# One unread product ahead of the up-projections of three feed-forward layers, and another order of products in the last chunks of the first

## What is computed

```python
def swiglu(x, w1, w3, w2):
    return (jax.nn.silu(x @ w1) * (x @ w3)) @ w2
...
        h = layer_norm(DN_ALPHA * h + m, ln_g[i, 0], ln_b[i, 0])
        h = layer_norm(DN_ALPHA * h + swiglu(h, ffn_w1[i], ffn_w3[i], ffn_w2[i]), ln_g[i, 1], ln_b[i, 1])
```

## Time and profile before

| | us |
|---|---|
| median of 3 runs | 1177.24 |
| lowest and highest | 1177.13, 1178.37 |
| span of the profiled execution, first to last instruction | 1173.9 |
| PE busy in it | 1157.0 |
| DVE, ACT, POOL busy in it | 818.7, 600.6, 160.6 |

### The profile page before, as it was taken

One profiled execution on the slowest core, in us unless ns is written; L12 is line 12 of the kernel. 1 busy time (PEld: TensorE's weight loads), 2 busy tenths in 40 slices (PEclk: granted clock), 3 DMA queues, 4 the chain that ended last, 5 costly groups with the idle time before them and its releaser, 6 DMA issues.

```text
span 1173.9 us, 20445 instructions
## 1 busy us (share of the span) xinstructions
PE 1157.0 (99%) x8266; PEld 1037.8 (88%) x8266; DVE 818.7 (70%) x1263; ACT 600.6 (51%) x947; POOL 160.6 (14%) x212
## 2 busy tenths in 40 slices
PE   9999999999999999999999999999999999999996
PEld 7997899999877789999998889999979988999996
DVE  7789899989868687455466785454577768655554
ACT  6777444544445456354434565444438664544441
POOL 0650199003960000000000000000010000000000
PEclk9999999999999999999999999999999999999999
DMA  6676454555765558565544557555536334755540
GB/s 250 219 280 220 145 202 157 198 180 180 219 176 191 183 192 307 171 216 190 187 162 161 197 200 231 198 181 196 180 125 228 116 111 159 269 195 183 195 147 36
DMA packets 63974, 221.02 MB, mean 188 GB/s; under 512 B 8068, under 2 KB 9988, under 8 KB 63368
## 3 DMA queue, kind: packets, MB, share of 16 engines
q1 hardware_dynamic: 57224, 202.57, 50.7%
q0 software_dynamic: 5648, 15.73, 4.0%
q10 hardware_dynamic: 1008, 1.41, 0.4%
HBM read 211.03 MB, written 7.60 MB: 186 GB/s over the span
## 4 chain that ended last, share of the span: by engine, by line
PE 88%; DVE 8%; DMA 2%; ACT 1%; issue 1%; SPq 0%; DVEq 0%; ACTq 0%
PE bank L1627 15%; PE bank L1628 15%; PE bank L1629 15%; PE bank L1636 8%; PE bank L1642 8%; PE bank L1638 8%; PE bank L1747 5%; PE bank L1681 4%; DVE wlo L1020 2%; DMA raw<-in_w 2%; PE bank L1936 1%; PE bank L1607 1%; PE bank L1782 1%; PE bank L1918 1%; PE bank L1947 1%
## 5 line engine op out<-in xcount | busy, mean ns | idle before, releaser
L1020 DVE TENSOR_TENSOR wlo<-raw,whi 128x1024 fp32r<-128x1024 f32 x227 | 287.4, 1272 | 57.0 <-ACT whi L616 55.9
L616 ACT ACTIVATE whi<-raw 128x1024 fp32r<-128x1024 f32 x227 | 238.9, 1056 | 71.8 <-PE bank L1642 41.0
L1627 PE MATMUL bank<-xboth,whi 128*128 128x256 f32 x936 | 264.2, 282 | 0.0
L1628 PE MATMUL bank<-xboth,whi 128*128 128x256 f32 x936 | 262.3, 280 | 0.0
L1629 PE MATMUL bank<-xboth,wlo 128*128 128x256 f32 x936 | 262.3, 280 | 0.0
L1020 DVE TENSOR_TENSOR ext<-raw,ext 128x1024 fp32r<-128x1024 f32 x142 | 172.2, 1222 | 39.0 <-ACT ext L616 38.7
L1629 PEld LDWEIGHTS bank<-xboth,wlo 128*128 128x128 f32 x936 | 178.7, 191 | 0.0
L1627 PEld LDWEIGHTS bank<-xboth,whi 128*128 128x128 f32 x936 | 176.0, 188 | 2.5 <-issue 0.9
L1628 PEld LDWEIGHTS bank<-xboth,whi 128*128 128x128 f32 x936 | 175.9, 188 | 1.4
L616 ACT ACTIVATE ext<-raw 128x1024 fp32r<-128x1024 f32 x142 | 148.5, 1055 | 43.4 <-DMA raw<-in_w 21.3
L1627 PE MATMUL bank<-xboth,ext 128*128 128x256 f32 x600 | 169.4, 282 | 0.3 <-ACT silu L697 0.3
(11 more groups left out here) (385 smaller groups left out, 1969.6 us busy)
## 6 DMA issues: line engine op xcount, KB each, us to landing
raw<-in_w SPq DMA_DIRECT2D x370, 512.0 KB, 4.1
slot<-in_ln_row POOLq DMA_DIRECT2D x16, 512.0 KB, 5.0
toep<-slot POOLq DMA_DIRECT2D x8, 512.0 KB, 8.2
toepA<-toep SPq DMA_DIRECT2D x2, 1024.0 KB, 5.8
BT<-toep SPq DMA_DIRECT2D x2, 1024.0 KB, 6.5
x_tm<-in_x SPq DMA_DIRECT2D x2, 512.0 KB, 4.9
slot<-in_s_B SPq DMA_DIRECT2D x2, 512.0 KB, 4.8
slot<-in_s_C SPq DMA_DIRECT2D x2, 512.0 KB, 5.2
```

Of the source, the lines that this page charges most:

```text
L616: nc.scalar.activation(hi_of(c), raw[:, c % RAW, :], ACT.Copy).then_inc(w_hi, 1)
L1020: V.tensor_tensor(lo_of(c), raw[:, c % RAW, :], hi_of(c).bitcast(F32), ALU.subtract).then_inc(w_lo, 1)
L1627: mm(dst, wh, bhi[:, kc, :], start=(i == 0), stop=False)
L1628: mm(dst, wh, blo[:, kc, :], start=False, stop=False)
```

## The change

Two functions are new, and two lines of `ffn` use them. `unread(l)` issues one product into bank 7 whose result nobody reads: in the second layer (l = 1) a transpose of 32 rows by 128 columns with 32 moving columns, in the third (l = 2) a transpose of 128 by 128, in the fourth (l = 3) a float32r product of 128 by 128 weights with 64 moving columns. In the first layer it issues nothing. It stands behind the waits of `up1(c)` and ahead of its first product, for c = 4 to 21. `fm_passes` issues the same 24 products as `fm` in another order: first the 8 of high by high, then the 8 of high weights by low activations, then the 8 of low weights by high activations. It takes the place of `fm` in both up-projections of the chunks 13 to 21 of the first layer.

```diff
+            def fm_passes(c, dst):
+
+                def weights(part, kc):
+                    return (hi_of(c), hi_of(c), lo_of(c))[part][:, kc * P:(kc + 1) * P]
+                for part in range(3):
+                    for kc in range(KC):
+                        ins = mm(dst, weights(part, kc), (xhi, xlo, xhi)[part][:, kc, :], start=part + kc == 0, stop=part == 2 and kc == KC - 1)
+                return ins
+
+            def unread(l):
+
+                if l == 1:
+                    nc.tensor.transpose(bank[7][:, 0:32], cst[0:32, 0:P], cst[0:32, 0:32])
+                if l == 2:
+                    nc.tensor.transpose(bank[7][:, 0:P], ident, ident)
+                if l == 3:
+                    mm(bank[7][:, 0:64], xhi[:, 0, 0:P], xhi[:, 0, 0:64], start=True, stop=True)
+
...
                     if c > 2:
                         pe.wait_ge(silu_ready, E0 + c)
-                    used(fm(u, bank[4][:, 0:SEQ], xhi, xlo))
+                    if c > 3:
+                        unread(l)
+                    used((fm_passes(u, bank[4][:, 0:SEQ]) if l == 0 and c >= 13 else fm(u, bank[4][:, 0:SEQ], xhi, xlo)))
...
-                    used(fm(u, bank[5][:, 0:SEQ], xhi, xlo))
+                    used((fm_passes(u, bank[5][:, 0:SEQ]) if l == 0 and c >= 13 else fm(u, bank[5][:, 0:SEQ], xhi, xlo)))
```

## The result

The kernel after takes 1184.54 us (median of 4 runs, 1184.27 to 1187.21), the kernel before 1177.18 us in 4 runs on the same chip. That is slower, where 1172.1 had been forecast and 1179.6 was the upper end of the range. The ratio of the two is 1.0077, with a 95% interval of 1.0064 to 1.0091, which stands for 7.5 to 10.7 us; the medians of these few runs lie 7.4 us apart. The profiled execution has a span of 1183.0 us and took 1184.8, so 1.8 us lie around the span. The 3.3 us that the prediction put between the span of before and its median were 1.8 of that kind and 1.5 of scatter between runs; the two spans, 1173.9 and 1183.0, differ by 9.1.

A forecast was written before the change was run, and what follows sets the result against it. PE was taken to bound the kernel, busy 1157.0 of 1173.9 us. Span 1173.9 less 3.54 (three layers) and 1.6 (passes) gave 1168.8; with 3.3 between span and median, 1172.1 us, range 1171.2 to 1179.6.

The forecast's parts named there:

- The two paces: In `fm`, the same 24 products run at 118 ns (slow) or 113 ns (fast) a product, at full clock.
- `down` sets the pace back: Behind every plain `down` at its steady 227 ns a product, the next two calls of `fm` are slow.
- The rule of the Trainium skill that the prediction weighed: Distance of products follows from columns and clock alone, 109 ns for 256 columns; given little weight.
- the price of the 32-row product: Layer two, chunks 4 to 21: 1.18 us gained; if slow, 0.12 to 0.14 us a place, 2.3 a layer.
- The step from 8 transposes to one: Layer three: a chunk behind one transpose is fast, 8.31 us against 8.37; 1.18 us gained in the layer.
- 64 columns: Layer four's unread product, chunks 4 to 21: turns the pace like a full transpose, 1.18 us gained.
- one of the small products does not turn its layer: Rival for layers two and four: 3.5 us more, 1175.6 or 1177.2 us; one layer staying slow had chance 0.27.
- better than even: The chance given to layers two and four to turn fast behind their small products.
- The passes: Layer one, chunks 13 to 21: 1.6 us gained by pass order; bounds 1.6 gained to 1.1 lost.
- the pooling mixer's third pace: `fm` over other tiles in the pooling mixer: 2.88 us a call, 120 ns; taken to show that operand sequence matters.
- the fifth case: None of the three layers turns, or the passes or another thing cost more; chance 0.12, outside the range.
- Nothing turns: Rival: all three layers stay slow, 54 products cost 6.9 us: 1184.1, or 1182.5 with the passes' gain; within chance 0.12.

## Why the prediction was wrong

**What held.** PE bounds the kernel: no wait for weights appeared in the changed stretches with 9 us more or 6 us less on PE, as the earlier trace rows had said. The two paces are real, and an unread product ahead of a call of `fm` can move it from the one to the other: the fast chunks of layer three have 8.30 and 2.72, where 8.31 and 2.72 had been forecast. `down` sets the pace back; the run with a single transpose shows it directly. The rule of the Trainium skill that the prediction weighed ("TensorE: Matmul & The Clock Gate", section "Back-to-back issue gap") is a formula from columns and clock for the isolated gap, and the section itself says that in a stream of loads and products both set the distance. As a forecast of one distance the formula fares no better than before: the same 256 columns at the same full clock stand 113 or 118 ns apart, by what went ahead.

**The step that cost most: the price of the 32-row product.** "so a short product hides nothing and saves nothing: I take the same 1.18 for each", with 0.12 to 0.14 a place if the pace stays slow. A place cost 0.41, and the layer 7.1 us where it was to gain 1.18. From the last product of `down` to the second of `fm` there are 0.32 + 0.17 + 0.22 = 0.71 us, where a plain entry has 0.227 + 0.118 = 0.345: 0.37 more. The other 0.04 lies in `down`, eleven distances of 0.231 instead of 0.227. The bounds came from loads with full rows. The 0.11 of the earlier trace rows is the distance between the starts of two loads, and the record of one load there is 0.19. The nearer row was in the trace of before, and it wasn't used for the bound: `u_turned` makes its transposes of 32 rows right behind a product of 512 columns (the row of L2007 holds two, the second of them at 349.89).

```profile
349.66 0.62 PE L2007 MATMUL bank<-whi,xboth 128*128 128x512 f32 x2
350.21 1.45 PE L2020 MATMUL bank<-cst,slot 32*128 32x32 f32 x24
```

The distance is 0.32 us, with no wait recorded and PEld idle for 0.36 just before, and the full product behind the last of them comes 0.15 later: the two gaps of the changed kernel, 0.32 and 0.17, to about 0.02 us. A bound by the length of a load says nothing of when the load begins, and that was the cost.

**The step from 8 transposes to one.** The saving for layer three was worked out from the earlier trace rows on the premise that a single transpose turns every chunk as the blocks of 8 do. The text named the gap ("though never behind a single one") and still gave the layer its full 1.18. Of the 16 entries from `down` half came out slow, and the two late ones as well: 8 x 0.07 gained and 10 x 0.11 lost, 0.5 lost instead of 1.2 gained. The text also leaned on "Behind full transposes all 16 entries are fast". Eight of these stand behind only two transposes, in the one execution that was read; in the other thirteen traces 38 of 104 such entries are fast.

**64 columns.** The rival "one of the small products does not turn its layer" was right here in mechanism and price: 16 x 0.13 = 2.1 us, less a little that the fast chunks 20 and 21 give back, 2.0 measured where 2.1 to 2.5 were forecast. What failed is the chance given to the turn, "better than even". The turn isn't a matter of a load ahead of `fm`.

**The passes.** No change is what the runs show, the middle of the bounds; the 1.6 taken on the likelier side was not there. The argument from the pooling mixer's third pace, that what is read after what matters, does not carry over to the order of the same operands.

**The outcome as a case.** It lies in the fifth case, given 0.12, "None turns, or the passes or another thing cost more", and by its time near the 1182.5 to 1184.1 of "Nothing turns", but that nearness is luck: layers three and four stay under the 2.3 us of a slow layer, and layer two costs three times as much. Each of the two failures gives the wrong sign by itself. With everything else as forecast, 7.1 us for layer two outweigh the 2 x 1.18 + 1.6 = 4.0 gained elsewhere; and with the forecast price of 2.3 for a slow layer two, the three layers would still have cost 2.3 + 0.5 + 2.0 = 4.8.

## What to carry to other kernels

When a string of small products runs a few per cent above its best distance at full clock, look at what stands directly ahead of the string: here one unread product of the same kind, with full rows and 256 columns, cost 0.12 us and won 0.18 in each chunk, and smaller ones of 128 and 192 columns turned the pace as well behind `down`. Look for the nearest row of each new kind of product in the trace you have, as the 32-row transposes stood there with their price, and look at more than one execution before you call a pace the rule. Give no product in the stream fewer rows than its neighbours without measuring it; the loads on both sides of it then come late. And try an edit at one place before counting it at 54: what held behind a block of 8 transposes held behind a single one half of the time.

## What the runs showed that was not expected

- A product whose weights have 32 or 64 rows, between full ones, starts 0.32 us behind a product of 512 columns instead of 0.227, and the next full one 0.17 to 0.22 behind it.
- The pace behind a single full transpose alternates from one transpose of a layer to the next, at distances from 8.3 to 17.0 us.
- The same code goes either way from one execution to the next where two transposes stand ahead of it (chunk 2: 46 calls fast, 66 slow in fourteen traces).
- Which products turn the pace does not follow their size in one direction: 64 no, 128, 192 and 256 yes, 320 and 512 no; with 32 rows 64 columns do. The fast distance, 2.72/24 = 113.3 ns, is half of `down`'s 2.72/12 = 226.7; the slow one, 117.8, is 4% more. What fixes the two is open.
- An unread product made the kernel faster, ratio 0.995, though PE is its bound and was already busy throughout.
